# Grid attention with its tokens laid out by columns: 512 keys for each query block, two heads at once

## What is computed

```python
GRID_W, CTX_LEN, HEAD_DIM, NA_HEADS, NA_COLS = 64, 256, 64, 16, 16     # rows = 512 // 64 = 8
def neighbourhood_mixer(...):
    kr = min(NA_ROWS_MAX, rows)                       # 8: every query sees all 8 rows
    row_start = jnp.clip(r_idx - kr // 2, 0, rows - kr)                 # always 0
    col_start = jnp.clip(col - NA_COLS // 2, 0, GRID_W - NA_COLS)
    col_in = (col[None, :] >= col_start[:, None]) & (col[None, :] < col_start[:, None] + NA_COLS)
    col_bias_idx = jnp.clip(col[None, :] - col[:, None], -(NA_COLS - 1), NA_COLS - 1) + NA_COLS - 1
    def row_block(args):
        s_loc = jnp.einsum('bqhd,brkhd->bhqrk', q_row, k_band).astype(jnp.float32) * ATTN_SCALE
        bias = rpb[:, row_off][:, :, col_bias_idx].transpose(0, 2, 1, 3)
        s_loc = jnp.where(col_in[None, None, :, None, :], s_loc + bias[None].astype(jnp.float32), -jnp.inf)
        s_ctx = jnp.einsum('bqhd,bkhd->bhqk', q_row, k_c).astype(jnp.float32) * ATTN_SCALE
        s_all = jnp.concatenate([s_loc.reshape(B, NA_HEADS, GRID_W, n_loc), s_ctx], axis=-1)
        prob = jax.nn.softmax(s_all, axis=-1).astype(v_band.dtype)
        o = einsum(prob over grid keys, v_band) + einsum(prob over context keys, v_c)
    o = lax.map(row_block, (q_rows, r_idx, row_start))
    y_l = o.swapaxes(0, 1).reshape(B, S, D_MODEL) @ w_o
```

## Time and profile before

| | |
|---|---|
| Median of 3 runs | 4331.46 us (4327.49 to 4334.54) |
| The profiled execution: its time, its span | 4335.81 us, 4334.0 us |
| TensorE busy, mean granted clock | 4029.7 us (93%), 0.952 |
| VectorE, ScalarE, GpSimd busy | 1845.5, 1441.6, 466.6 us |
| Second layer's attention, groups 0 to 3 | start at 1321.1, 1442.6, 1562.3, 1681.9, end at 1793.2 us |

### The profile page before, as it was taken

How to read it: one execution, slowest core, us unless ns; L and a number is a source line. 1 busy time by engine, 2 the same in 40 slices (tenths; PEclk the granted TensorE clock), 3 DMA queues, 4 the chain that set the end, 5 groups by cost and what they waited for, 6 DMA issues and landing times.

```text
span 4334.0 us, 66723 instructions
## 1 busy us (share of the span) xinstructions
PE 4029.7 (93%) x28114; PEld 3570.8 (82%) x28114; DVE 1845.5 (43%) x3401; ACT 1441.6 (33%) x2876; POOL 466.6 (11%) x529
## 2 busy tenths in 40 slices
PE   6988899999989999899989989979997998997998
PEld 6866678888878777788878869979996886997998
DVE  3443454323334444544445444343335544434344
ACT  3444443212233333332322343333232224434322
POOL 1211120000012222100010000020002000002001
PEclk8988899999989999999999979989998998998999
DMA  4022112222331110133311102322321110222332
GB/s 165 25 88 83 52 39 72 98 98 98 98 107 44 35 34 28 40 103 101 103 53 40 49 18 69 91 63 89 93 83 44 40 45 23 77 91 65 93 93 74
DMA packets 86762, 303.75 MB, mean 70 GB/s; under 512 B 9392, under 2 KB 12592, under 8 KB 86336
## 3 DMA queue, kind: packets, MB, share of 16 engines
q1 hardware_dynamic: 84944, 292.72, 21.5%
q0 software_dynamic: 1520, 6.75, 0.5%
HBM read 297.34 MB, written 2.10 MB: 69 GB/s over the span
## 4 chain that ended last, share of the span: by engine, by line
PE 87%; ACT 5%; DVE 3%; POOL 2%; issue 2%; DMA 2%; ACTq 0%; SPq 0%; DVEq 0%; POOLq 0%
PE bank L472 58%; PE bank L534 6%; PE bank L954 3%; PE bank L825 2%; PE bank L503 2%; PE bank L803 2%; PE bank L943 2%; PE bank L740 1%; POOL scratch L2402 1%; PE bank L779 1%; PE bank L1046 1%; PE bank L624 1%; PE bank L813 1%; PE bank L1019 1%; PE bank L685 1%
## 5 line engine op out<-in xcount | busy, mean ns | idle before, releaser
L1688 DVE TENSOR_TENSOR weight_lo<-weight_raw,weight_hi 128x1024 fp32r<-128x1024 f32 (+1 forms) x464 | 561.5, 1214 | 564.3 <-ACT weight_hi L1123 564.1
L472 PE MATMUL bank<-u_hi,weight_hi 128*128 128x256 f32 (+1 forms) x2368 | 692.3, 292 | 8.0 <-DVE u_lo L2342 5.8
L472 PE MATMUL bank<-u_lo,weight_hi 128*128 128x256 f32 (+1 forms) x2368 | 678.4, 286 | 0.0
L472 PE MATMUL bank<-u_hi,weight_lo 128*128 128x256 f32 (+1 forms) x2368 | 677.6, 286 | 0.0
L1123 ACT ACTIVATE weight_hi<-weight_raw 128x1024 fp32r<-128x1024 f32 (+1 forms) x464 | 476.3, 1031 | 504.9 <-PE bank L472 370.6
L472 PE MATMUL bank<-h_hi,weight_hi 128*128 128x512 f32 (+1 forms) x1360 | 500.1, 368 | 24.2 <-DVE h_lo L2073 12.9
L472 PE MATMUL bank<-h_lo,weight_hi 128*128 128x512 f32 (+1 forms) x1360 | 478.4, 352 | 0.0
L472 PE MATMUL bank<-h_hi,weight_lo 128*128 128x512 f32 (+1 forms) x1360 | 478.0, 351 | 0.0
L472 PEld LDWEIGHTS bank<-u_hi,weight_hi 128*128 128x128 f32 x2368 | 454.8, 192 | 27.4 <-issue 17.6
L472 PEld LDWEIGHTS bank<-u_hi,weight_lo 128*128 128x128 f32 x2368 | 454.8, 192 | 0.0
L472 PEld LDWEIGHTS bank<-u_lo,weight_hi 128*128 128x128 f32 x2368 | 453.7, 192 | 0.1
(11 more groups left out here) (270 smaller groups left out, 7587.3 us busy)
## 6 DMA issues: line engine op xcount, KB each, us to landing
weight_raw<-in_w_mlp SPq DMA_DIRECT2D x128, 512.0 KB, 3.6
weight_raw<-in_w_ff SPq DMA_DIRECT2D x128, 512.0 KB, 3.6
weight_raw<-in_w_in SPq DMA_DIRECT2D x92, 512.0 KB, 3.6
weight_raw<-in_w_mod SPq DMA_DIRECT2D x80, 512.0 KB, 3.9
weight_raw<-in_a_w_qkv SPq DMA_DIRECT2D x24, 512.0 KB, 4.3
weight_raw<-in_b_w_qkv SPq DMA_DIRECT2D x24, 512.0 KB, 3.6
first_weight<-in_w_mod SPq DMA_DIRECT2D x16, 512.0 KB, 14.7
weight_raw<-in_w_ret_o SPq DMA_DIRECT2D x16, 512.0 KB, 3.6
```

What stands on the lines that cost most here:

```text
L472: m = e.matmul(view[:, 0:hi - lo], a[:, k, :], b[:, k0 + k, lo:hi], start=(k == 0 and i == 0), stop=(k == kt - 1 and i == 2))
L1688: e.tensor_tensor(wlo[s][:, 0:kt, :], raw[n % N_RAW][:, 0:kt, :], whi[s][:, 0:kt, :].bitcast(F32), ALU.subtract).then_inc(*tick("dve_split ...
```

## The change

The latent tokens come from the host ordered by column (8 rows of column 0, then of column 1, and so on), with the rotary tables to match. A block of 128 queries is then 16 columns, and all its keys lie in 32 columns: 256 grid keys and 256 context keys, 512 in place of 768.

- `NEAR` has 8 units in a group in place of 16. A unit is two heads (s = 0, 1) and one block. Their scores use rows 0 to 63 and rows 64 to 127 of the array; they are written in pieces where the key columns don't lie in a row (4, 6, 6 or 2 products for the four blocks).
- The weights are divided by their sum before the transposes (`expo` on DVE, two 128x512 multiplications), and the eight transposes serve both heads.
- Values: v is the stationary operand (64 columns), the turned weights move (128 wide); head s writes partitions 64 s to 64 s + 63. The result is already turned, so L835, L2058 and the output rows go. ACT writes it to `attn_out_T` back in row order.
- `V_EDGE`: two more ACT copies of half the partitions for each group's v.
- POOL: 12 small bands a group (128x256, 128 KB each, fetched in pairs into eight buffers, one addition each) in place of 4 large ones. After group 0, `to_rows` puts the residual in row order for the later layers: 8 times a copy to `weights_T` and a copy back, 128x512 each.

```diff
-        NEAR = [(tt, qt, sub) for tt in range(2) for sub in range(2) for qt in range(4)]
+        NEAR = [(tt, qt) for tt in range(2) for qt in range(4)]
@@ tensor_program, near_units
-                    for part, (a, c) in enumerate(ALL.spans):
-                        job = ("s", 1, g, i, part)
-                        view = take(*job)
-                        e.matmul(view[:, 0:c - a], QK[b][r, tt, P * qt:P * qt + P], QK[b][r, 2 + tt, a:c],
-                                 start=True, stop=True).then_inc(*tick(("pe_scoreu", "pe_scorel")[sub], job))
+                    for to, (a, c) in pieces:
+                        for s in range(2):
+                            r = slice(HD * s, HD * s + HD)
+                            m = e.matmul(views[s][:, to:to + c - a], QK[b][r, tt, P * qt:P * qt + P],
+                                         QK[b][r, 2 + tt, a:c], start=True, stop=True)
...
-                    for k in range(6):
-                        m = e.matmul(view[:, 0:HD], WT[:, P * k:P * k + P], V[b][:, k, v0:v0 + HD],
-                                     start=(k == 0), stop=(k == 5))
+                    for k, v in enumerate(near_values(b, qt)):
+                        for s in range(2):
+                            v0 = P * tt + HD * s
+                            m = e.matmul(view[HD * s:HD * s + HD, 0:P], v[:, v0:v0 + HD], NWT[s][:, P * k:P * k + P],
+                                         start=(k == 0), stop=(k == 3))
@@ vector_program, near_units
+                def expo(i):
+
+                    for s in range(2):
+                        e.wait_ge(*at("w", 1, g, i, s))
+                    e.reciprocal(small(i, 4, 2), small(i, 2, 2)).then_inc(*tick("dve_attn", ("rc", 1, g, i)))
                     e.wait_ge(*at("rc", 1, g, i))
...
+                    for s in range(2):
+                        x = NS[i % 2][s]
+                        e.tensor_scalar(x, x, small(i, 4 + s), None, ALU.mult).then_inc(
+                            *tick("dve_attn", ("n", 1, g, i, s)))
@@ pool_program
+            def to_rows():
+
+                for k in range(KT):
+                    x, tmp = X[:, k, N_META:N_META + N_LAT], WT[:, 0:N_LAT]
...
+                    e.tensor_copy(tmp.rearrange("p (r c) -> p c r", c=GRID_W),
+                                  x.rearrange("p (c r) -> p c r", r=8)).then_inc(*tick("pool_norm", ("gridx", k)))
+                    e.wait_ge(*at("gridx", k))
+                    e.tensor_copy(x, tmp).then_inc(*tick("pool_norm", ("grid", k)))
@@ pool_program, attention_layer
+                    if (layer, g) == (1, 0):
+                        to_rows()
```

226 lines of the change are left out of this document (120 added, 106 removed).

## The result

The changed kernel takes **4178.95 us** (median of 4 runs, 4165.79 to 4188.14), the kernel before beside it 4333.0. In two later sets of runs the same kernel took 4180.07 and 4181.95 us (0.9643 and 0.9648). The profiled executions are 4335.8 and 4188.1 us, 147.7 apart.

A forecast was written before the change was run, and what follows sets the result against it. TensorE's own work was taken to bound groups 0 to 2. Savings of 96 - 4 (`to_rows`) - 3 (clock) + 27.5 (last group) + 1 (its end) = 117.5 us, from 4331.5, gave 4214 us; range 4195 to 4244.

The forecast's parts named there:

- The halves run together: TensorE's scores and values: two heads overlap on array halves; the rival that they don't gave 4260 us, chance 0.05.
- the chain doesn't take TensorE's place: Denies the rival that each unit waits for ACT's copies or DVE's normalisation: 38 us back, 4252 us, chance 0.13.
- `to_rows` is not slow: Denies the rival of 2.5 us a POOL copy, stalling 28 us around group 1's start: 4238 us, chance 0.06.
- the rivals on the slower side: Chain bounds 4252 (0.13), halves apart 4260 (0.05), slow `to_rows` 4238 (0.06), fill and chain without overlap 4405 us (0.01).
- better: Rival: no copy waits, `to_rows` hidden, full clock at group starts, `h_lo` sooner: 20 us more, 4194 us, chance 0.08.
- the price of a pair before: TensorE's scores, transposes, values and half an L835 for two heads in the old kernel: 6.96 us.
- The products of a pair: TensorE's attention products for two heads fall from 6.96 to 3.1 us, saving 3.86 for each of 32 pairs.
- Waits of groups 0 to 2: TensorE's time without work stays even: about 4.4 us a group after, 4.8 before.
- a loss of 4 us: Group 1's start, once: TensorE waits at the second unit's transposes for a band delayed by `to_rows` (bounds 0 and 8).
- They are two weights ahead, which covers this: Group 1: the `weight_lo` splits behind DVE's wait for the band were to cost TensorE nothing.
- The last group: 32 us saved, less 6.5 for its start and 2 for lower clock, plus 4 for fewer waits: 27.5 us.
- 3 us for groups' starts: New waits at three group starts may bring stretches at the lower clock, costing 3 us.

The follow-up runs named there:

- full_between: Changed kernel with head 0's products first, then one whole-array transpose of the identity, then head 1's, in scores and values: 4253.08 us.
- full_before: Changed kernel with the same extra whole-array transposes ahead of both heads, which alternate as in the changed kernel: 4180.33 us.
- before_one_slot: Kernel before, with the projections' products handed out at one place a unit, between transposes and what follows: 4313.36 us, ratio 0.9953.
- no_middle_products: Changed kernel with the projections' products at two places a unit, none between transposes and values: 4208.59 us.
- again: The changed kernel, same code, run once more: 4180.07 us, ratio 0.9643 to the kernel before.
- before_two_slots: Kernel before, with the projections' products at two places a unit, ahead of and behind the transposes, not three: 4337.5 us, ratio 1.0007.
- earlier_two_slots: Changed kernel with row-order copies spread over group 1, earlier `h_lo`, and the projections' products at two places a unit: 4163.48 us, ratio 0.9604.

## Why the prediction fell short

**The bound was right.** TensorE's own work set groups 0 to 2 and a unit's chain through VectorE and ScalarE the last group's start. The halves run together (`full_between` against `full_before`), the chain doesn't take TensorE's place (no wait in the steady state, 80.6 us a group), `to_rows` is not slow, `h_lo` is what the last group waits for. None of the rivals on the slower side came; "better" came, and 15 us more than it. Two steps failed: the price of a pair before, which was taken from one unit, and what becomes of the waits on ScalarE's copies.

**The products of a pair: 3.86 us forecast, 4.26 measured** (57.7 less 23.6 over 8; 15.5 us too little over all four groups). Before, I read 6.96 us out of one unit; the sum over the group is 7.21, and it doesn't hold the 0.2 of entry that my 6.96 has, since the table counts it with the product ahead of the scores. Scores were right (2.95 for two; 2.98 without entry in the earlier trace rows), but transposes are 0.69 each and not 0.58, values 1.35 and not 1.26, L835 0.10 and not 0.05. The unit of the earlier trace rows has products on every side and the full clock, and I had taken it for all. In group 1 the five units with no product behind their transposes take 0.65 to 0.82 us for them, waits left out, and one in the stretch at 1.2 GHz takes 1.17. The values take 1.26 between products, 1.36 behind a wait, 1.38 where the next scores follow at once, and 1.48 with both. After, the forecast was 3.1, entry included, and the measured 2.95 without it: scores 1.10 for the same 1.1, transposes 0.85 for 0.83, values 1.00 for 1.08. In the last group the saving is 36.2 us for 30.9: there the pairs of before took 3.9 us more than in group 2, at the lower clock and with more waits behind them, those of after 1.8.

**Waits of groups 0 to 2: "even", measured 3.4, 0.4 and 3.1 us less.** This is the other step that failed. I kept "2 of the 4 us of waits on ACT's copies" and added 2.4 at the group's start. What I didn't count is where these waits stood. All but 0.4 us a group of them stood in units with nothing between transposes and values, as `before_one_slot` and `no_middle_products` show from both sides. Three places a unit with half as many units double each place's share, to 2.0 us, and no place between transposes and values is empty. So all 12.5 us went, in place of half. The start was costed well: 0.9 ahead of the first transposes (forecast 1.5), 0.7 for the keys' scaling (0.9).

**`to_rows`: forecast a loss of 4 us, measured 3.** The two `again` profiles have group 1 at 83.5 and 83.6 us beside 80.8; the 84.8 of the first profile holds a further 1.2 of lower clock. The copies took less than forecast, 14.6 us for 17.6, and began 8.1 us ahead of group 1 for 7:

```profile
L2570 POOL COPY weights_T<-residual 128x512 f32<-128x512 f32 x8 | 8.8, 1099 | 0.4
L2573 POOL COPY residual<-weights_T 128x512 f32<-128x512 f32 x8 | 5.0, 623 | 0.5
```

The path was another than forecast. VectorE waited for the band 4.3 us, not 9, and TensorE's wait was not at the second unit's transposes but on `weight_lo`, behind VectorE's wait:

```profile
DVE scratch L2065 <- POOL band L2548: 4.3, 2, 2.8
```

"They are two weights ahead, which covers this" was wrong by 2.5 us. The writing side pays for a wide step here: 1.10 us for a copy that writes in steps of 256 bytes beside 0.62 for the contiguous one of the same size. The Trainium skill (GPSIMD Engine Reference, Performance pitfalls for Q7 kernels) says this of reading alone, at half as much again; here, in writing, it is 76% more. I had set 8 us of loss beside that case; it didn't follow, because the other eight copies took 0.62 and not 1.0.

**The last group: forecast 27.5 us less and 1 more at its end, measured 37.1.** `h_lo` was there 13.2 us behind the first score (forecast 14.1), with 9.2 us idle ahead of it and not 11. In the rest of the group the table has 8.3 us of idle time before and 2.2 after, where I had 7.4 and 3.5; what is left is a single wait of 2.2 for `h_lo` at the end, which before had as well (2.3). The 2 us for more products at the lower clock didn't come: a mean of 0.94 over 111.3 us and of 0.91 over 75.2 us are both some 13.5 us at 1.2 GHz. The pairs gave 5.3 us more than 30.9. The rest of the products gave 0.2 for 1.3.

**The clock: 3 us for groups' starts didn't come.** A wait of 0.9 us at a start brings no lower level; groups 0 and 2 stand at 1.00. On the contrary, the kernel before had a short stretch at the lower level in each group, 13.6 us in groups 0 to 2 together in its first profile, and the changed one has none in five of the six groups 0 to 2 of `again` and the first profile, and 3.4 us in the sixth. At half the clock each of these costs up to half its length, so some 5 us of what the pairs and the rest gave in groups 0 to 2 is clock (an estimate from these stretches), which the forecast had no term for. My reason was the last group, where three waits of 1.44 to 1.66 us follow one another within 8 us; a single one of 0.9 is another case.

In short: 15.5 us for the pairs, 13.9 for idle time and 5 for the clock make up the 35. Most choices between two bounds were taken on the cautious side, and such errors don't average out.

## What to carry to other kernels

Before you say what becomes of a wait, list where it stands: here all but 0.4 us a group of it stood at units with no other work between transposes and values, and a change that doubles the work at each such place removed it altogether. Giving all the filler work to that one place was worth 20 us without any other change; by its profile 2.7 of the 6.8 us a group were idle time, the rest time of the products themselves. Take a price from the sum over a whole group, start to start, and not from one clean unit. To test whether two halves of the array run together, put a product on the whole array between them; the order of the instructions alone didn't keep them apart here.

## What the runs showed of the hardware

- Products on different halves of the array start out of the program's order. With all eight passes of head 0 ahead of head 1's in the program, head 1 starts 0.49 us later and not 0.87 or more, beside head 0's fifth pass; putting the heads one behind the other costs 3.7 us a group in the values, 1.1 in the scores and 10.3 us in the kernel's time, where keeping them apart costs 7.8 and 7.8 a group.
- Two heads on two halves take as long as one: 1.02 us for 8 passes of one or 16 of two (`full_between`, `full_before`).
- The granted clock differed with how the same products are spread: 1.00 in groups 1 and 2 of `before_one_slot`, 0.96 to 0.99 in groups 0 to 2 of the kernel before, 0.94 and 0.92 to 0.93 in groups 1 and 2 of both profiles of `before_two_slots`, at the price of 3 to 6 us a group. The engine was busy for 96 to 98% of the group in all of them. This took away what that edit had gained. Why it differs isn't shown.
- A change between shapes of products is cheap: two places a unit for three (`earlier_two_slots`), eight interruptions fewer a group, save 1.0 of the 48.1 us that a group's projections take.
